# First feed-forward panel on values not yet normalised, with its correction on VectorE, and a banded rotation read from PSUM

## The reference, cut to what matters

```python
def layer_norm(x, g, b):
    mu = jnp.mean(xf, axis=-1, keepdims=True)
    var = jnp.mean(jnp.square(xf - mu), axis=-1, keepdims=True)
    return (xf - mu) * lax.rsqrt(var + LN_EPS) * g + b
...
    for i in range(DEPTH):
        ...                      # mix = the mixer of this layer, on h
        h = layer_norm(DEEPNORM_ALPHA * h + mix, ln1_g[i], ln1_b[i])
        ffn = conv_glu_ffn(h, ffn_w_in[i], ffn_conv_w[i], ffn_conv_b[i], ffn_w_out[i], valid)
        h = layer_norm(DEEPNORM_ALPHA * h + ffn, ln2_g[i], ln2_b[i])
```

## Time and profile before

| what | value |
|---|---|
| median of 3 runs | 1307.65 us (1306.29 to 1307.88) |
| profiled execution, its own time | 1306.24 us |
| its span, first to last instruction | 1304.4 us |
| TensorE matmul busy | 1282.8 us (98%) |
| VectorE busy | 925.3 us (71%) |
| ScalarE busy | 810.2 us (62%) |
| GpSimd busy | 224.0 us (17%) |
| weight units moved | 379 of 512 KB, 203.22 MB in all |
| mean granted clock of TensorE | 0.997 |

### The profile page before, as it was taken

The page is one execution under the profiler, slowest core; times in us unless marked ns, Lnnn a source line. Parts: engine busy times, 40 slices in busy tenths (PEclk is TensorE's granted clock), DMA queues, the critical chain, the costliest instruction groups (busy, mean ns, idle before and its releaser), DMA issues.

```text
span 1304.4 us, 29971 instructions
## 1 busy us (share of the span) xinstructions
PE 1282.8 (98%) x10367; PEld 1236.9 (95%) x10367; DVE 925.3 (71%) x1889; ACT 810.2 (62%) x1683; POOL 224.0 (17%) x212
## 2 busy tenths in 40 slices
PE   9999999999998999999999999999999999999997
PEld 8999999999987999999987899999999999999997
DVE  5766877765797877775668687776567767777764
ACT  5576666654577676664477766665446775766653
POOL 1000144420000034430000003442000000334400
PEclk9999999999999999999999999999999999999999
DMA  7433456556421456556542145555645434456572
GB/s 287 146 103 123 134 179 191 176 182 192 130 85 61 145 179 185 182 163 209 164 130 86 43 152 179 191 177 179 193 145 154 125 115 130 155 185 191 178 228 80
DMA packets 57444, 203.22 MB, mean 156 GB/s; under 512 B 6416, under 2 KB 8624, under 8 KB 57232
## 3 DMA queue, kind: packets, MB, share of 16 engines
q1 hardware_dynamic: 57104, 201.68, 49.3%
q0 software_dynamic: 256, 0.41, 0.1%
HBM read 200.61 MB, written 1.05 MB: 155 GB/s over the span
## 4 chain that ended last, share of the span: by engine, by line
PE 83%; DVE 8%; ACT 4%; issue 2%; POOL 1%; DMA 0%; ACTq 0%; DVEq 0%; SPq 0%; POOLq 0%
PE ps L406 23%; PE ps L409 22%; PE ps L410 22%; PE ps L588 2%; DVE w_lo L1317 2%; PE ps L569 2%; PE ps L450 1%; PE ps L456 1%; PE ps L453 1%; POOL gated L1291 1%; DVE scores L1377 1%; PE ps L555 1%; ACT probs L930 1%; ACT w_hi L880 1%; DVE probs L1395 1%
## 5 line engine op out<-in xcount | busy, mean ns | idle before, releaser
L1317 DVE TENSOR_TENSOR w_lo<-raw,w_hi 128x1024 fp32r<-128x1024 f32 (+1 forms) x379 | 460.9, 1217 | 215.5 <-ACT w_hi L880 209.8
L406 PE MATMUL ps<-h_hi,w_hi 128*128 128x272 f32 (+1 forms) x1752 | 508.6, 290 | 1.1 <-DVE w_lo L1317 0.6
L410 PE MATMUL ps<-h_hi,w_lo 128*128 128x272 f32 (+1 forms) x1752 | 501.5, 286 | 0.0
L409 PE MATMUL ps<-h_lo,w_hi 128*128 128x272 f32 (+1 forms) x1752 | 500.6, 286 | 0.0
L880 ACT ACTIVATE w_hi<-raw 128x1024 fp32r<-128x1024 f32 x375 | 393.5, 1051 | 140.0 <-PE ps L406 127.9
L406 PEld LDWEIGHTS ps<-h_hi,w_hi 128*128 128x128 f32 x1752 | 329.1, 188 | 7.9 <-issue 5.4
L409 PEld LDWEIGHTS ps<-h_lo,w_hi 128*128 128x128 f32 x1752 | 329.4, 188 | 0.3
L410 PEld LDWEIGHTS ps<-h_hi,w_lo 128*128 128x128 f32 x1752 | 328.6, 188 | 0.0
L406 PE MATMUL ps<-hid_hi,w_hi 128*128 128x272 f32 (+2 forms) x636 | 182.9, 288 | 0.6 <-DVE w_lo L1317 0.5
L1291 POOL TENSOR_TENSOR gated<-y 128x272 f32<-128x272 f32 x88 | 134.6, 1529 | 273.7 <-DVE y L1749 259.5
L410 PE MATMUL ps<-hid_hi,w_lo 128*128 128x272 f32 (+2 forms) x636 | 181.5, 285 | 0.0
(11 more groups left out here) (191 smaller groups left out, 1711.6 us busy)
## 6 DMA issues: line engine op xcount, KB each, us to landing
raw<-in_weights SPq DMA_DIRECT2D x375, 512.0 KB, 3.6
cst<-in_consts SPq DMA_DIRECT2D x1, 1586.5 KB, 9.9
h<-in_x SPq DMA_DIRECT2D x4, 272.0 KB, 4.2
raw<-in_weights SPq DMA_DIRECT2D x4, 256.0 KB, 4.5
out<-h SPq DMA_DIRECT2D x8, 128.0 KB, 1.7
v_tok<-v_tok POOLq DMA_DIRECT2D x6, 64.0 KB, 3.7
cst<-in_consts SPq DMA_DIRECT2D x1, 209.0 KB, 6.1
v_tok<-v_tok POOLq DMA_DIRECT2D x2, 8.0 KB, 2.2
```

Of the source, the lines that this page charges most:

```text
L406: m = pe.matmul(b, whi, xhi, start=n == 0, stop=False)
L409: pe.matmul(b, whi, xlo, start=False, stop=False)
L410: m = pe.matmul(b, wlo, xhi, start=False, stop=n == len(tiles) - 1)
L1317: return dve.tensor_tensor(out_, a_, b_, op)
```

## The change

Three things are changed.

1. For the four norms behind a mixer (`RAW_NORMS`), panel 0 of "up" is computed from g * h, without mean and variance (`raw_panel`), in place of the filler matmuls. ScalarE and VectorE make the high and low part of g * h chunk by chunk during the output stage (`raw_hi_done`, `raw_lo`). Two more columns, g and b, run along, so that the panel holds W'(g h), W'g and W'b. After the norm's last low part VectorE forms rstd * (W'(g h) - mean * W'g) + W'b in four steps into `fixed_panel`, which the activation and the convolution of panel 0 read. Panels 1, 2 and 3 are led behind it (`leading_behind_raw`). The unit for panel 3 is split in two halves around the norm (`late_half`). The last unit that the output stage splits comes ahead of the last join on VectorE.
2. In all norms VectorE centres chunks 0 to 3 and GpSimd chunks 4 to 7.
3. In swa the two products of the rotation read the panel from PSUM (`turn_parts`), the swap matmul takes the sine product, and the addition reads its result from PSUM; `rope` and the scaled copy go, and the scale moves into the mask. ScalarE copies the transposes ahead of the first exponential. The third panel's first matmuls come ahead of the last two transposes.

```diff
-CENTER_DVE = 6
+CENTER_DVE = 4
...
+RAW_NORMS = (0, 2, 4, 6)
...
+        fixed_panel = totals[:, 0, :]
+        def next_stage(n):
+            return LAYERS[(n + 1) // 2][NEXT[n]]
+        def norm_cols(n):
+            return ln_par[:, n].rearrange("p two k -> p k two")
+        def late_cols(half):
+            return slice(half * UNIT // 2, (half + 1) * UNIT // 2)
...
+            def raw_panel(n):
+                r = RAW_NORMS.index(n)
+                s, u0, p0 = next_stage(n)
+                t0 = LAST_FROM[NEXT[n]] if (n + 1) // 2 == DEPTH - 1 else 0
+                b, slot = ps[:, p0 % BANKS, t0:T + 2], u0 % RING
+                pe.wait_ge(lo_ready, u0 + 1)
+                pe.wait_ge(cols_ready, r + 1)
+                for k in range(DC):
+                    pe.wait_ge(raw_split, DC * r + k + 1)
+                    whi, wlo = (w[slot][:, k * P:(k + 1) * P] for w in (w_hi, w_lo))
+                    xhi, xlo = (x_part[:, k, t0:T + 2] for x_part in (h_hi_row, h_lo_row))
+                    m = pe.matmul(b, whi, xhi, start=k == 0, stop=False)
+                    if k == 0:
+                        m.then_inc(w_used, 1)
+                    pe.matmul(b, wlo, xhi, start=False, stop=False)
+                    m = pe.matmul(b, whi, xlo, start=False, stop=k == DC - 1)
+                    m.then_inc(raw_read if k < DC - 1 else panel_done, 1)
+            def leading_behind_raw(n, u0, p0, t0):
+                r = RAW_NORMS.index(n - 1)
+                js = range(1, BANKS)
+                slots = {j: (u0 + j) % RING for j in js}
+                banks = {j: bank(p0 + j)[:, t0:T] for j in js}
+                for k in range(DC):
+                    at_k = slice(k * P, (k + 1) * P)
+                    pe.wait_ge(norm_hi, DC * n + k + 1)
+                    if k == DC // 2:
+                        pe.wait_ge(lo_ready, u0 + BANKS)
+                    if k < DC - 1:
+                        for j in js:
+                            if k == 0 and j < BANKS - 1:
+                                pe.wait_ge(lo_ready, u0 + j + 1)
+                            elif k == 0:
+                                pe.wait_ge(late_lo, r + 1)
+                            m = pe.matmul(banks[j], w_hi[slots[j]][:, at_k], h_hi[:, k, t0:T], start=k == 0, stop=False)
+                            if k == 0 and j == 1:
+                                m.then_inc(w_used, 1)
+                            pe.matmul(banks[j], w_lo[slots[j]][:, at_k], h_hi[:, k, t0:T], start=False, stop=False)
+                        pe.wait_ge(h_ready, DC * n + k + 1)
+                        for j in js:
+                            pe.matmul(banks[j], w_hi[slots[j]][:, at_k], h_lo[:, k, t0:T], start=False, stop=False)
+                pe.wait_ge(h_ready, DC * n + DC)
+                for j in js:
+                    m = pe.matmul(banks[j], w_hi[slots[j]][:, at_k], h_hi[:, DC - 1, t0:T], start=False, stop=False)
+                    if j > 1:
+                        m.then_inc(w_used, 1)
+                    pe.matmul(banks[j], w_hi[slots[j]][:, at_k], h_lo[:, DC - 1, t0:T], start=False, stop=False)
+                    pe.matmul(banks[j], w_lo[slots[j]][:, at_k], h_hi[:, DC - 1, t0:T],
+                              start=False, stop=True).then_inc(panel_done, 1)
...
+                            elif j == 0 and name == "up" and 2 * layer in RAW_NORMS:
+                                leading_behind_raw(2 * layer + 1, u0, p0, t0)
...
-                if n < 2 * DEPTH - 1:
+                if n in RAW_NORMS:
+                    raw_panel(n)
+                elif n < 2 * DEPTH - 1:
...
+                if k == O_LED and kind == "swa":
+                    third_panel(a, range(0, 3))
...
-                if k == O_LED:
+                if k == O_LED and kind != "swa":
...
-                            swap(queries[:, m - 1, :], pq + m)
+                            swap(y[:, 1, :], pq + m)
...
-                            swap(q_rope[:, 0, :], pv + 2, 6)
+                            swap(y[:, 3, :], pv + 2, 6)
...
-                gemm(a, "up", from_h, norm_ready(2 * a + 1), lead=3)
+                gemm(a, "up", from_h, norm_ready(2 * a + 1), lead=BANKS if 2 * a in RAW_NORMS else 3)
...
+                if n in RAW_NORMS:
+                    if k == 0:
+                        act.activation(h_hi_row[:, :, T:T + 2], norm_cols(n), ACT.Copy).then_inc(cols_hi, 1)
+                    act.activation(h_hi[:, k, :], h[:, k, :], ACT.Identity,
+                                   scale=ln_par[:, n, 0, k:k + 1]).then_inc(raw_hi_done, 1)
+            def late_half(n, half):
+                _, u0, p0 = next_stage(n)
+                u, slot = u0 + AHEAD, (u0 + AHEAD) % RING
+                act.wait_ge(raw_landed[slot], (u // RING + 1) * 16)
+                act.wait_ge(panel_done, p0)
+                act.activation(w_hi[slot][:, late_cols(half)], raw[slot][:, late_cols(half)],
+                               ACT.Copy).then_inc(hi_ready if half else late_hi, 1)
...
+                if n in RAW_NORMS:
+                    late_half(n, 0)
...
+                if n in RAW_NORMS:
+                    late_half(n, 1)
                 for k in range(DC):
+                    if n in RAW_NORMS and k < DC - 1:
+                        act.wait_ge(raw_read, (DC - 1) * RAW_NORMS.index(n) + k + 1)
+                    elif n in RAW_NORMS:
+                        act.wait_ge(panel_done, next_stage(n)[2] + 1)
...
-                        if m >= 2:
-                            exps(a, kind, 2 * m - 4)
...
+                            exps(a, kind, 2 * m - 4)
...
                             for u in units_of(a, "up", i, j):
-                                split_hi(u)
+                                if least or j or 2 * a not in RAW_NORMS:
+                                    split_hi(u)
...
-                            act.activation(y[:, j, :], bank(pu + j), ACT.Identity,
+                            source = bank(pu + j)
+                            if not least and j == 0 and 2 * a in RAW_NORMS:
+                                act.wait_ge(fixed, RAW_NORMS.index(2 * a) + 1)
+                                source = fixed_panel
+                            act.activation(y[:, j, :], source, ACT.Identity,
...
+                if n in RAW_NORMS:
+                    pool.wait_ge(raw_split, DC * RAW_NORMS.index(n) + DC)
...
-                            split_units(layer, name, i, j)
+                            if not (name == "up" and isinstance(i, int) and j == 0):
+                                split_units(layer, name, i, j)
...
+                elif name == "up" and 2 * layer in RAW_NORMS:
+                    turn(0)
+                    turns(dve, s.turns, turn, first=1)
...
-            def rope(qn, swap_no, cos, sin, dst, rows=P, where=7):
-                tt(y[0:rows, 0, :], qn[0:rows], cos[0:rows], ALU.mult)
-                dve.wait_ge(swapped, swap_no)
-                own.link(tt(y[0:rows, 1, :], ps[0:rows, where, 0:T], sin[0:rows], ALU.mult))
-                return tt(dst, y[0:rows, 0, :], y[0:rows, 1, :], ALU.add)
...
-                        in1=mask[0:r, cols], scale=q_scale[0:r, ch:ch + 1] if kind == "mla" else -1.0,
+                        in1=mask[0:r, cols], scale=q_scale[0:r, ch:ch + 1] if kind == "mla" else
+                        -SCALE["swa"] if kind == "swa" else -1.0,
...
+                is_raw = n in RAW_NORMS
+                r = RAW_NORMS.index(n) if is_raw else 0
+                def raw_lo(k):
+                    dve.wait_ge(raw_hi_done, DC * r + k + 1)
+                    dve.scalar_tensor_tensor(h_lo[:, k, :], h[:, k, :], ln_par[:, n, 0, k:k + 1],
+                                             h_hi[:, k, :].bitcast(F32), ALU.mult, ALU.subtract).then_inc(raw_split, 1)
+                def late_half(half):
+                    slot = (next_stage(n)[1] + AHEAD) % RING
+                    cols = late_cols(half)
+                    if half:
+                        dve.wait_ge(hi_ready, next_stage(n)[1] + AHEAD + 1)
+                    else:
+                        dve.wait_ge(late_hi, r + 1)
+                    tt(w_lo[slot][:, cols], raw[slot][:, cols], w_hi[slot][:, cols].bitcast(F32),
+                       ALU.subtract).then_inc(lo_ready if half else late_lo, 1)
...
-                    if 2 <= k < DC - 1:
+                    if 2 <= k < DC - (not is_raw):
...
+                    if is_raw and k == 1:
+                        dve.wait_ge(cols_hi, r + 1)
+                        tt(h_lo_row[:, :, T:T + 2], norm_cols(n), h_hi_row[:, :, T:T + 2].bitcast(F32),
+                           ALU.subtract).then_inc(cols_ready, 1)
+                    if is_raw and k:
+                        raw_lo(k - 1)
...
-                gemm(n // 2, stage, join, links=None, before=before, straight=True, late=add_last)
+                gemm(n // 2, stage, join, links=None, before=before, straight=True, late=None if is_raw else add_last)
```

(37 more changed lines are left out.)

9 lines of the change are left out of this document (7 added, 2 removed).

## The result

The changed kernel takes 1318.07 us (median of 4 runs, 1317.04 to 1318.48), the kernel before 1307.62 (4 runs on the same chip): a ratio of 1.0079, 95% interval 1.0066 to 1.0092. It is 10.4 us slower. The direction was forecast, the size was not: 1310.9 was predicted, and 1318.1 lies above the range. The profiled execution took 1318.29 us, its span is 1316.5, 12.1 more than before (12.0 between the unrounded spans).

A forecast was written before the change was run, and what follows sets the result against it. TensorE, busy for 98% of the span, was taken as the bound, VectorE in the sliding-window layer. Terms +8.3 + 1.7 - 5.6 - 1.1 = +3.3 us gave 1310.9 us from a median of 1307.65; range 1303 to 1316.

The forecast's parts named there:

- Part 1: Four raw mixer norms: VectorE's added work makes panel 5 late by 2.07 us each, +8.3 us in all.
- Part 1, ahead of the exponential: Output stage: 4.13 us added on VectorE against 1.88 idle; last join 2.25 us later, exponential 2.05 later.
- Part 1, behind it: From the exponential to panel 5: centrings moved off VectorE, correction added; panel 5 2.07 us later in all.
- Part 1, the fourth norm: Norm n = 6: taken to look like the other mixer norms to 0.3 us, so also +2.07 us.
- the clock's term: Idle gap between led panels and panel 4: clock falls at two gaps in four, 0.85 us each, +1.7 us.
- Part 2: Sliding-window layer: VectorE is the bound; less rotation work, a new order and a steadier clock give -5.6 us.
- Part 3: All norms: two more centrings on GpSimd save VectorE time without slowing its rescalings, -1.1 us.
- The end of the kernel: Last norm: the end hangs on VectorE, and two centrings of 0.35 us leave the chain, -0.7 us.
- (b): Rival: GpSimd blocks VectorE in four raw norms and the last, clock falls after all four gaps: 1316.6 us; chance 0.08.
- (a): Rival: VectorE's added work is absorbed, each raw norm costs 0.4 us: 1303.2 us, faster; chance 0.20.
- (c): Rival: sliding-window layer stays bound by mask, exponential and normalisation, gives only 3 us: 1313.5 us; chance 0.15.
- (d): Rival: the stretches cancel, raw norms cost 1.5 us each, clock kept: 1307.0 us, no change; chance 0.17.

The follow-up runs named there:

- e4: Changed kernel with six chunks centred on VectorE again instead of four: 1315.97 us, ratio 1.0068 to the kernel before.
- e7: e4 with filler matmuls in TensorE's idle time ahead of the sums and behind the led panels of the raw norms: 1313.38 us, ratio 1.0051.
- e9: Kernel before with only the order of the sliding-window layer changed, old rotation and centring kept: 1304.71 us, ratio 0.9976.
- e8: Kernel before with the rotation's two products from PSUM, old sliding-window order, no raw norms, centring as before: 1309.08 us, ratio 1.0014.
- e3: Kernel before with four chunks centred on VectorE instead of six, nothing else changed: 1310.3 us, ratio 1.0021.
- e6: e4 without the three VectorE steps that correct panel 0: 1309.37 us, ratio 1.0017.
- e11: Changed kernel, six centrings on VectorE, units for panels 4 to 6 split ahead of the correction, ScalarE's bias steps on h late: 1311.82 us, ratio 1.0031.
- e2: Changed kernel without raw norms and with six chunks centred on VectorE, so only the sliding-window part is left: 1303.09 us, ratio 0.9971.

## Why the prediction was wrong

**Part 1, ahead of the exponential.** The working held. VectorE's first join of the stage was already 0.41 us later than before. From there its last join came 1.96 later, where 4.13 us against 1.88 idle had given 2.25, and the exponential 2.00, where I had 2.05.

**Part 1, behind it.** From the exponential to panel 5 I had +0.02 and measured +0.57: the blocked rescalings. Counted from the last matmul of the output stage, a norm at full clock cost 2.36 (n = 0) and 2.39 (n = 4) instead of 2.07: 0.3 too little.

**Part 1, the fourth norm: the first step that failed.** I wrote that the four norms look alike to 0.3 us and multiplied by four. They were alike while TensorE set the pace. In the last layer TensorE's matmuls are narrower (258 columns, one every 0.12 us instead of 0.125), VectorE's instructions are not, so VectorE is further behind: the wait ahead of the sums is 2.11 us instead of 1.53. Behind it the clock fell while the sums ran, where nothing hides it, and the norm cost 5.20. By e4 and e7 about 1.5 of that is the clock; 1.3 is left over the 2.4 of the other norms. I had put the clock's term (+1.7 in all) only behind the led panels. In the trace that gap (2.2 us three times, 2.5 in the last layer) was followed by a fall once, at 459.5 to 462.9, and by none in the other three. Where it fell, panel 4 ran at 1.2 GHz, panel 5 came straight behind it without a wait, and the norm cost 2.88, about 0.5 more than its like (I had 0.85). The clock's size in all, some 2.0 us, was near, but three quarters of it came in another place. In sum Part 1 came to 12.8 us against 10.0.

**Part 2.** -4.54 us against -5.6. The price was near, and about 0.9 of it is the fall of the clock that the trace of before has at this layer's end and the new one has not. The reason was only half right. I read "VectorE is the bound" from 6.69 busy of 6.90 us. e9 shows that VectorE's own work does hold a pair at 6.87. But e8 shows a second limit beside it, a ring through ScalarE and VectorE of 6.90: taking work off VectorE outside the ring gave nothing, and adding to the ring cost 0.35. The prediction counted 0.35 us in seven pairs for the products; without the new order they would have lost as much. The earlier trace rows could not tell the two limits apart: ScalarE waits 1.12 us for the mask while VectorE never idles, which fits both.

**Part 3: the second step that failed.** I had -1.1 and it came to about +1.4 in the traces (0.78, 0.51 and 0.13), and in the medians 2.1 to 3.8. The end of the kernel, which was to gain 0.7, lost 0.13. The argument was that a rescaling "has never taken over 552 ns" while GpSimd centres. But in the trace of before GpSimd's two centrings began at 139.6 and ran 0.77 each (all of them, in that trace):

```profile
L1267 POOL TENSOR_TENSOR h<-h,y x16: 761/768/781, 139.6 to 1296.5; 128x272 f32<-128x272 f32 x16
```

They were over at about 141.1, and the first rescaling began at 140.8: the two met for 0.3 us, once in a norm. The maximum was the sign: it is always this rescaling, the first of a norm, that is long (541 to 552 ns in seven norms, 520 in the last). With four centrings the overlap is two whole instructions, and the second rescaling takes 1000 to 1015 ns in six norms; in the last mixer norm the first two take 1014 and 998. The Trainium skill (SBUF — State Buffer, Who interferes with whom) says that a VectorE instruction with two SBUF inputs and a GpSimd instruction that reads SBUF exclude each other; the 1015 ns here and the 1004 of e3 agree with it, and so do the 1.12 us of three centrings, whose second input is in PSUM. I had read the row that spoke against it as a test, though the two hardly met in it.

**The rest.** 2.3 us were in no term. The last panel ahead of the first norm came 0.62 later, which varies from kernel to kernel (0.25 earlier in e6, 0.70 later in e11, with the same instructions of TensorE ahead of it), and the pairs of up and down stages took 0.27 to 0.55 longer each. In the trace a turn of four up panels takes 12.107 us instead of 12.053 in two of the three full layers, with the same instructions. Both values come in kernels with and without raw norms, and in different layers of one kernel (in e2: 12.053, 12.053, 12.107). What sets it was not found.

**The rivals.** (b), at 0.08, named the two things that happened, GpSimd blocking VectorE and a falling clock, and at 1316.6 was the nearest in time. It was priced low for the row of 552 ns. (a) fell: beyond its idle time, VectorE absorbed nothing of the added work. (c) named three members of the ring and 3 us; the layer gave 4.54, or some 3.6 without the clock. (d) had 1.5 for a raw norm, and none cost less than 2.36.
